# Prompt attention scores as two query tiles side by side in 64-row tiles of TensorE, with three products in place of four

## What is computed

```python
z = jnp.einsum('bqhd,bkhd->bhqk', q.astype(jnp.float32), k.astype(jnp.float32)) * (HEAD_DIM ** -0.5)
z = z + sb_bias.astype(jnp.float32)[None, :, None, None]
mask = kpos[None, :] < qpos[:, None]
l = jnp.where(mask, jax.nn.log_sigmoid(-z), 0.0)
later = jnp.flip(jnp.cumsum(jnp.flip(l, -1), -1), -1) - l
w = jnp.where(mask, jnp.exp(jax.nn.log_sigmoid(z) + later), 0.0)
return jnp.einsum('bhqk,bkhd->bqhd', w, v.astype(jnp.float32)).astype(q.dtype)
```

## Time and profile before

| | us |
|---|---|
| median of 3 runs (2441.89 to 2444.11) | 2442.11 |
| profiled execution, span | 2440.8 |
| PE busy in it | 2406.7 |
| PEld busy | 2331.5 |
| DVE busy | 1585.0 |
| ACT busy | 1286.6 |
| POOL busy | 243.0 |

### The profile page before, as it was taken

One profiled execution on the slowest core, in us unless ns is written; L12 is line 12 of the kernel. 1 busy time (PEld: TensorE's weight loads), 2 busy tenths in 40 slices (PEclk: granted clock), 3 DMA queues, 4 the chain that ended last, 5 costly groups with the idle time before them and its releaser, 6 DMA issues.

```text
span 2440.8 us, 36724 instructions
## 1 busy us (share of the span) xinstructions
PE 2406.7 (99%) x13263; PEld 2331.5 (96%) x13263; DVE 1585.0 (65%) x2233; ACT 1286.6 (53%) x1982; POOL 243.0 (10%) x527
## 2 busy tenths in 40 slices
PE   7999999999999999999999999999999999999998
PEld 7999999999999999999999999999999999999998
DVE  7635662656777787777788777757655665764335
ACT  5466523555655745656555565554455555444432
POOL 0012320200001100011100111000122130000000
PEclk9999999999999999999999999999999999999999
DMA  8434554534444434444443443333566674343332
GB/s 257 153 108 143 159 174 138 184 111 130 162 134 139 142 110 144 150 129 144 128 124 117 137 141 124 125 122 114 182 187 187 209 234 134 120 136 117 112 118 83
DMA packets 141526, 351.64 MB, mean 144 GB/s; under 512 B 20625, under 2 KB 64146, under 8 KB 141218
## 3 DMA queue, kind: packets, MB, share of 16 engines
q1 hardware_dynamic: 128994, 312.88, 40.6%
q0 software_dynamic: 12352, 36.42, 4.7%
HBM read 300.11 MB, written 49.12 MB: 143 GB/s over the span
## 4 chain that ended last, share of the span: by engine, by line
PE 95%; DVE 2%; ACT 2%; DMA 1%; issue 1%; SPq 0%; DVEq 0%; ACTq 0%
PE PS L1136 22%; PE PS L1138 22%; PE PS L1137 22%; PE PS L874 5%; PE PS L872 5%; PE PS L873 5%; PE PS L942 2%; PE PS L964 1%; PE PS L932 1%; PE PS L963 1%; PE PS L1026 1%; PE PS L933 1%; PE PS L1056 1%; PE PS L1014 1%; PE PS L912 1%
## 5 line engine op out<-in xcount | busy, mean ns | idle before, releaser
L1440 ACT ACTIVATE w_hi_lo<-w_raw 128x1024 fp32r<-128x1024 f32 x240 | 252.7, 1053 | 283.5 <-PE PS L1138 277.3
L1136 PE MATMUL PS<-a_hi,w_hi_lo 128*128 128x416 f32 x1080 | 385.1, 357 | 1.3 <-DVE w_hi_lo L1995 1.3
L1138 PE MATMUL PS<-a_hi,w_hi_lo 128*128 128x416 f32 x1080 | 379.3, 351 | 0.0
L1137 PE MATMUL PS<-a_lo,w_hi_lo 128*128 128x416 f32 x1080 | 378.6, 351 | 0.0
L1995 DVE TENSOR_TENSOR w_hi_lo<-w_raw,w_hi_lo 128x1024 fp32r<-128x1024 f32 x240 | 292.6, 1219 | 58.1 <-ACT w_hi_lo L1440 55.9
L1136 PE MATMUL PS<-h_hi,w_hi_lo 128*128 128x416 f32 x824 | 294.6, 358 | 0.0
L1138 PE MATMUL PS<-h_hi,w_hi_lo 128*128 128x416 f32 x824 | 290.2, 352 | 0.0
L1137 PE MATMUL PS<-h_lo,w_hi_lo 128*128 128x416 f32 x824 | 289.4, 351 | 0.0
L2022 DVE TENSOR_TENSOR h_lo<-h_full,h_hi 128x416 fp32r<-128x416 f32 x160 | 94.6, 592 | 222.9 <-ACT h_hi L1455 222.8
L1136 PEld LDWEIGHTS PS<-a_hi,w_hi_lo 128*128 128x128 f32 x1080 | 203.0, 188 | 4.1 <-DVE w_hi_lo L1995 1.7
L1137 PEld LDWEIGHTS PS<-a_lo,w_hi_lo 128*128 128x128 f32 x1080 | 203.5, 188 | 2.1
(11 more groups left out here) (336 smaller groups left out, 5203.8 us busy)
## 6 DMA issues: line engine op xcount, KB each, us to landing
w_raw<-w_all SPq DMA_DIRECT2D x380, 512.0 KB, 3.5
proj_scratch<-stage SPq DMA_DIRECT2D x70, 208.0 KB, 1.9
k_rows<-kv_out SPq DMA_DIRECT2D x80, 128.0 KB, 4.0
v_hi_lo<-v_scratch SPq DMA_DIRECT2D x40, 256.0 KB, 4.1
x_scratch<-x_full SPq DMA_DIRECT2D x20, 416.0 KB, 2.9
x_residual<-x_scratch SPq DMA_DIRECT2D x5, 1664.0 KB, 7.6
pages<-ck SPq DMA_DIRECT2D x64, 128.0 KB, 2.2
pages<-ck POOLq DMA_DIRECT2D x64, 128.0 KB, 2.5
```

Of the source, the lines that this page charges most:

```text
L1136: pe.matmul(out, w_h, mh_[:, k, :], start=(g == 0), stop=False)
L1137: pe.matmul(out, w_h, ml_[:, k, :], start=False, stop=False)
L1138: ins = pe.matmul(out, w_l, mh_[:, k, :], start=False, stop=(g == KT - 1))
L1440: act.activation(halves(w_hi(n)), raw_halves(n), ACT.Copy).then_inc(s_wh, 1)
```

## The change

- `scores(t)` is called in even slots only and makes the scores of units `t` and `t + 1`, six matmuls over 64 rows each. Unit `t` lies in partitions 0 to 63 and goes to bank 6, unit `t + 1` in partitions 64 to 127 and goes to bank 4 (`z_bank`). The three products are Q high by K high, Q high by K low, Q low by K high; low by low is left out. The two units alternate: product 1 of `t`, product 1 of `t + 1`, product 2 of `t`, and so on. In the built program the six are tiles of 64 rows by 128 columns of the array, at row 0 and at row 64, where the two of before were tiles of 128 by 128.
- `qs` holds the high part in columns 0 to 255 and the low part in 256 to 511, with tiles 0 and 2 of a chunk in the lower partitions and 1 and 3 in the upper. `load_q` fetches each row once; ScalarE and VectorE make the parts as 128x256 (before 128x512 and 64x512).
- V is turned into bank 6, in slots 25, 41, 61, 81 and 111 (before 24, 40, 60, 80, 110). `turn_v` waits for the sigmoids of the unit before; the next pair of scores waits for VectorE's low part of V.

```diff
-V_AT_SLOT = {24: 3, 40: 4, 60: 5, 80: 6, 110: 7}
+V_AT_SLOT = {25: 3, 41: 4, 61: 5, 81: 6, 111: 7}
...
+def z_bank(t):
+
+    return 4 if t % 2 else 6
...
                 if t:
                     pe.wait_ge(s_sn, t)
+                if t - 1 in V_TURNED:
+                    pe.wait_ge(s_vlo, V_TURNED[t - 1] + 1)
                 c, h, a = SETS[v]
-                q = qs[:, (c * NH + h) % 2, i * P:(i + 1) * P]
-                pe.matmul(PS[:, 6, 0:w], q, khl[:, v % 2, 0, 0:w], start=True, stop=False)
-                pe.matmul(PS[:, 6, 0:w], q, khl[:, v % 2, 1, 0:w], start=False, stop=True).then_inc(s_z, 1)
+                for q_low, k_low in ((0, 0), (0, 1), (1, 0)):
+                    for d in range(2):
+                        rows, w = slice(HD * d, HD * d + HD), unit(t + d)[2]
+                        at_ = q_low * 2 * P + i // 2 * P
+                        ins = pe.matmul(PS[:, z_bank(t + d), 0:w], qs[rows, (c * NH + h) % 2, at_:at_ + P],
+                                        khl[rows, v % 2, k_low, 0:w], start=(q_low + k_low == 0), stop=(q_low == 1))
+                        if q_low:
+                            ins.then_inc(s_z, 1)
...
-            def turn_v(m):
+            def turn_v(m, tau):

                 pe.wait_ge(s_vin2, 16 * (m + 1))
-                if m:
-                    pe.wait_ge(s_vlo, m)
+                pe.wait_ge(s_sn, tau)
...
-                if tau < N_UNITS:
+                if tau < N_UNITS and tau % 2 == 0:
                     scores(tau)
```

More of the change, by code:

```diff
@@ L219 @@
 V_AT_STEP = {78: 0, 81: 1, 83: 2}
-V_AT_SLOT = {24: 3, 40: 4, 60: 5, 80: 6, 110: 7}
+V_AT_SLOT = {25: 3, 41: 4, 61: 5, 81: 6, 111: 7}
+V_TURNED = {**{2 * (j - 78) + 1: m for j, m in V_AT_STEP.items()}, **V_AT_SLOT}
 def v_made(h, a):
@@ L657, in load_q @@
                 rows = proj_d[AT[Q, h // 2], HD * (h % 2):HD * (h % 2) + HD, c * CHW:(c + 1) * CHW]
+                rows = rows.rearrange("p (two half q) -> p half two q", half=2, q=P)
                 if w:
@@ L660, in load_q @@
                 for half in range(2):
-                    sp.dma_start(qst[HD * half:HD * half + HD, :], rows).then_inc(s_qin, 16)
+                    sp.dma_start(qst[HD * half:HD * half + HD, 0:2 * P].rearrange("p (two q) -> p two q", q=P),
+                                 rows[:, half]).then_inc(s_qin, 16)
             def load_k(v):
@@ L865, in project @@
                         if j in V_AT_STEP:
-                            turn_v(V_AT_STEP[j])
+                            turn_v(V_AT_STEP[j], 2 * (j - 78) + 1)
                         for tau in amid:
@@ L921, in scores @@
             def scores(t):
-                v, i, w, top = unit(t)
+                v, i, _, _ = unit(t)
                 if i == 0:
@@ L943, in turn @@
                 ins.then_inc(s_tr, 1)
-            def turn_v(m):
+            def turn_v(m, tau):
                 pe.wait_ge(s_vin2, 16 * (m + 1))
-                if m:
-                    pe.wait_ge(s_vlo, m)
+                pe.wait_ge(s_sn, tau)
                 for j in range(4):
-                    ins = pe.transpose(PS[:, 4, j * P:(j + 1) * P], vmk[:, 0, j, :].bitcast(F32), ident[:, :])
+                    ins = pe.transpose(PS[:, 6, j * P:(j + 1) * P], vmk[:, 0, j, :].bitcast(F32), ident[:, :])
                 ins.then_inc(s_vtr, 1)
@@ L973, in attention @@
                 if tau in V_AT_SLOT:
-                    turn_v(V_AT_SLOT[tau])
+                    turn_v(V_AT_SLOT[tau], tau)
                 if tau % 4 == 2 and 0 <= (tau - 6) // 4 < N_SETS:
@@ L1371, in round_q @@
                     act.wait_ge(s_z, 4 * FIRST[w - 1])
-                act.activation(qs[:, w % 2, :], qst[:, :], ACT.Copy).then_inc(s_qhi, 1)
+                act.activation(qs[:, w % 2, 0:2 * P], qst[:, 0:2 * P], ACT.Copy).then_inc(s_qhi, 1)
             def round_k(v):
@@ L1383, in round_v @@
                 act.wait_ge(s_vtr, m + 1)
-                act.activation(vmk[:, :, :, 0:HD], PS[:, 4, :].rearrange("p (j h d) -> p h j d", h=2, d=HD), ACT.Copy).then_inc(s_vhi, 1)
+                act.activation(vmk[:, :, :, 0:HD], PS[:, 6, :].rearrange("p (j h d) -> p h j d", h=2, d=HD), ACT.Copy).then_inc(s_vhi, 1)
             def sigmoids(t):
@@ L1394, in sigmoids @@
                     act.wait_ge(s_tr, t - 2)
-                act.activation(sP[:, t % 3, 0:w], PS[:, 6, 0:w], ACT.Sigmoid, scale=HD ** -0.5, bias=bias_h[:, h:h + 1])
+                act.activation(sP[:, t % 3, 0:w], PS[:, z_bank(t), 0:w], ACT.Sigmoid, scale=HD ** -0.5, bias=bias_h[:, h:h + 1])
                 if t >= 5:
@@ L1398, in sigmoids @@
                     act.wait_ge(s_car, t)
-                act.activation(nP[:, t % 5, 0:w], PS[:, 6, 0:w], ACT.Sigmoid, scale=-HD ** -0.5, bias=nbias_h[:, h:h + 1]).then_inc(s_sn, 1)
+                act.activation(nP[:, t % 5, 0:w], PS[:, z_bank(t), 0:w], ACT.Sigmoid, scale=-HD ** -0.5, bias=nbias_h[:, h:h + 1]).then_inc(s_sn, 1)
             def round_w(t):
@@ L1929, in round_q @@
                 dve.wait_ge(s_qhi, w + 1)
-                dve.tensor_tensor(qs[HD:P, w % 2, :], qst[HD:P, :], qs[HD:P, w % 2, :].bitcast(F32), ALU.subtract).then_inc(s_qlo, 1)
+                dve.tensor_tensor(qs[:, w % 2, 2 * P:4 * P], qst[:, 0:2 * P], qs[:, w % 2, 0:2 * P].bitcast(F32),
+                                  ALU.subtract).then_inc(s_qlo, 1)
             def round_k(v):
@@ L1939, in round_v @@
                 dve.wait_ge(s_vhi, m + 1)
-                dve.tensor_tensor(vmk[:, :, :, HD:P], PS[:, 4, :].rearrange("p (j h d) -> p h j d", h=2, d=HD),
+                dve.tensor_tensor(vmk[:, :, :, HD:P], PS[:, 6, :].rearrange("p (j h d) -> p h j d", h=2, d=HD),
                                   vmk[:, :, :, 0:HD].bitcast(F32), ALU.subtract).then_inc(s_vlo, 1)
```

## The result

| kernel | median us | runs | ratio to before | 95% interval |
|---|---|---|---|---|
| before | 2443.11 | 4 | | |
| changed | 2458.91 (2456.46 to 2459.94) | 4 | 1.0062 | 1.0049 to 1.0074 |

The changed kernel is 15.8 us (0.62%) slower. The forecast was 2472.5, 1.2% slower, with a range from 2450 to 2510: the direction, the range and the mechanism hold but for one term, and the loss is about half of what the sum said.

A forecast was written before the change was run, and what follows sets the result against it. TensorE, busy 99% of the span, was taken as the bound. 2440.8 + 30.1 (pairs) + 2.0 (V waits) - 1.7 (waits gone) gave 2471.2 us of span, 2472.5 median; range 2450 to 2510, the forecast's own 2453 to 2482.

The forecast's parts named there:

- TensorE sets the end: Whole kernel: TensorE is busy 99% of the span, so a microsecond of its time in the slots is one of span.
- A visit drains the array: At each of 80 score pairs: going to 64-row tiles and back drains TensorE, 0.09 us on either side.
- the rival without a drain (faster): Score pairs: 64-row tiles don't drain and loads hide under the other half's stream; 2428 to 2433 us, chance 0.14.
- 32-row pair: Two matmuls over 32 rows ending each sample of the sample attention; their round to another tiling and back cost 0.32 us.
- The halves stream together: Full score pair: both array halves stream at once, 0.69 us instead of 0.92; no row showed it.
- the rival in series: Score pairs: the two halves stream one after the other, +65.2 us, 2507.6 us in all; chance 0.20.
- The load of the upper half: Start of a full score pair: upper half's weights load after the lower's on one load path, 0.11 us more.
- The transposes' first load: After each score pair: the first transpose's weight load, hidden before, now shows and costs 0.11 us.
- The low bound: Score pairs with a measured 0.32 us round and all else hidden: 1.01, 1.01 and 0.68 us, +11.6 us in all.
- The wait for V: Scores after V-turning slots wait for VectorE's low part of V: some 0.65 us each, 3.3 at most, +2.0 taken.
- The three waits of 1.7 us that go: Odd slots 21, 69 and 121: scores no longer wait there for ScalarE's sigmoids, -1.7 us.
- The signs: Profile checks: first transpose 1.1 to 1.2 us after first score load; wrong if last dense start to transpose is under 1.1 or over 1.5.

The follow-up runs named there:

- A visit alone: Kernel before, with only each unit's second score matmul (Q by low K) cut to rows 0 to 63: 2496.12 us against 2443.50.
- each visit more: Changed kernel with an even slot's transposes moved between first and second product of its pair, 79 returns to 64-row tiles more: 2488.79 us, ratio 1.0186.

## Why the prediction was right, and where its sum was off

- **TensorE sets the end.** Right; what an experiment added to its queue or took from it came out in the time.
- **A visit drains the array.** Right, and the rival without a drain (faster) fell. The gap before the scores' first load is the forecast 0.09 us. A visit alone costs 0.33 (160 of them +52.6 us) where the 32-row pair had shown 0.32, though from other loads. That a change of columns is free while a change of rows is not, as read in the earlier trace rows, carried over to 64 rows.
- **The halves stream together.** Right, and I had called it the weakest link. With all six in one half the time is 2503.19, near the 2507.6 that the rival in series gave; the changed kernel is 44.3 us below that.
- **The load of the upper half, 0.11 us behind the lower.** Wrong. I took "one load path" from two loads of 128-row tiles. Loads of different rows begin at once. This took 0.11 too much into each wide pair and 0.33 into each narrow one, where I had six loads in a row: 64 x 0.11 + 16 x 0.33 = 12.3 us of the 16.0 us by which the forecast +30.1 stood over +14.1.
- **The transposes' first load, 0.11, "which before was hidden".** Too large. From the transposes' first step to the second dense matmul behind them were 0.63 us before and are 0.68 now. They were held by their loads anyway, so only 0.05 shows: 80 x 0.06 = 4.8 us. With the term above this makes 17.1, a little more than the gap; the terms were read at 0.01 us.
- **The low bound.** The measured pairs (1.05, 1.04 and 0.68 us) lie at the end of the range that I had set by the measured round with all loads hidden (1.01, 1.01 and 0.68). The row of a whole round trip was the better guide than the sum of its parts, in part by chance, since its loads were others. The upper end of the forecast's own range, 2482, had no sum behind it.
- **The wait for V.** Right: 0.19 us in slot 62, 0.92 in 82 and 0.59 in 112, 1.7 in all against 2.0.
- **The three waits of 1.7 us that go.** They went, and 1.6 us came back at the transposes of slots 69 (1.36) and 119 (0.28). I had asked what the scores wait for, and not what stands behind them in TensorE's queue when they are gone.
- **The signs.** From the last dense start to the first transpose are 1.18 us in slot 80, inside the 1.1 to 1.5 that I had set as the limits of being right. From the first load of the scores to the first transpose are 0.90, not the 1.1 to 1.2 that I had named: the step with the loads one behind the other is what fails there. The idle loads and the waits for V (three, 1.7 us) are as named.

## What to carry to other kernels

Smaller tiles side by side pay only when what they save in one visit is more than the price of going to another row tiling and back, here a third of a microsecond; three products for two units of 512 columns save 0.23. So gather as many of them as the banks allow in one visit, or leave them at 128 rows. No run here has two pairs in one visit; by the numbers of the full pair my estimate is 0.36 + 6 x 0.23 = 1.74 us against 1.84 for the same four units over 128 rows. Where a wait goes from the head of a queue, look at the next instruction behind it, since the engine that was late is still late.

## What was not expected of the hardware

- Loads and matmuls of the two halves run side by side: in a narrow pair, where nothing else holds them, the loads begin in twos, 0.11 us apart, and in a full pair six 64-row matmuls of 512 columns take 0.90 us from first load to the next tiling's load, against 1.57 in one half.
- The order in the queue doesn't matter between the halves: three products of one half and then three of the other took the same time as alternating ones (2458.89 and 2458.91 us).
- The drain before a change of rows is the same, 0.09 us, for tiles of 32 rows and of 64. What a visit costs depends on the load behind the drain too: 0.33 us where transposes follow, and 0.38 for each visit more where dense work follows.
